# The loop over the experts of a mixture layer, with its backward branch announced at its head

## The reference

```python
N_EXPERTS = 8
TOP_K = 2
D_FF_EXPERT = 7 * D_MODEL // 2

def moe_swiglu(h, router_w, router_b, w_gate, w_up, w_down):
    logits = jnp.einsum('bsd,de->bse', h, router_w) + router_b
    top_vals, top_idx = lax.top_k(logits, TOP_K)
    top_w = jax.nn.softmax(top_vals, axis=-1)
    combine = jnp.sum(jax.nn.one_hot(top_idx, N_EXPERTS) * top_w[..., None], axis=-2)
    y = jnp.zeros_like(h)
    for e in range(N_EXPERTS):
        y = y + combine[..., e:e + 1] * swiglu(h, w_gate[e], w_up[e], w_down[e])
    return y
```

## Time and profile before

| what | us |
|---|---|
| median of 3 timed runs | 2754.07 (2751.21 to 2754.27) |
| the profiled execution | 2757.03 |
| its span, first to last instruction | 2755.2 |
| PE busy | 2518.5 (91%) |
| DVE, ACT, POOL busy | 669.3, 339.0, 58.5 |
| mixture of experts, first to last matmul | 1628 to 2744 |

### The profile page before, as it was taken

One profiled execution on the slowest core, in us unless ns is written; L12 is line 12 of the kernel. 1 busy time (PEld: TensorE's weight loads), 2 busy tenths in 40 slices (PEclk: granted clock), 3 DMA queues, 4 the chain that ended last, 5 costly groups with the idle time before them and its releaser, 6 DMA issues.

```text
span 2755.2 us, 27500 instructions
## 1 busy us (share of the span) xinstructions
PE 2518.5 (91%) x11186; PEld 1582.3 (57%) x11187; DVE 669.3 (24%) x1491; ACT 339.0 (12%) x905; POOL 58.5 (2%) x95
## 2 busy tenths in 40 slices
PE   8999899999999999999998988759998687979797
PEld 5565466656664666657776654339974343434343
DVE  0353200013532343453334621111010101010101
ACT  1242000001420000110001011001000000000001
POOL 0000000000000000000000000000000000000000
PEclk9999999999999999999999989989989898999899
DMA  5323334333234867336664279893657896759771
GB/s 209 124 96 130 141 123 153 137 128 127 92 115 168 336 244 258 116 130 260 254 269 160 81 321 431 362 407 150 262 230 317 364 429 281 304 230 403 295 309 62
DMA packets 71346, 620.35 MB, mean 225 GB/s; under 512 B 4096, under 2 KB 4096, under 8 KB 48816
## 3 DMA queue, kind: packets, MB, share of 16 engines
q1 hardware_dynamic: 57344, 557.33, 51.0%
q0 software_dynamic: 13728, 60.14, 5.7%
q10 hardware_dynamic: 144, 0.90, 0.1%
HBM read 617.31 MB, written 1.05 MB: 224 GB/s over the span
## 4 chain that ended last, share of the span: by engine, by line
PE 81%; DMA 8%; issue 5%; DVE 4%; ACT 2%; POOL 1%; ACTq 0%; DVEq 0%; POOLq 0%; SPq 0%
PE G L1907 8%; DMA big<-in_moe_pack 7%; PE S L2105 7%; PE G L1680 6%; PE S L2103 6%; PE G L1696 5%; PE S L1900 4%; PE T L1900 4%; PE G L2118 4%; PE G L1877 3%; PE S L2040 3%; PE T L2040 3%; PE G L2116 3%; PE G L2046 2%; PE G L1887 2%
## 5 line engine op out<-in xcount | busy, mean ns | idle before, releaser
L2103 PE MATMUL S<-big,hT 128*64 128x256 f32 x2240 | 280.0, 393 | 89.7 <-issue 49.7
L2103 PEld LDWEIGHTS S<-big,hT 128*64 128x64 f32 x2240 | 160.6, 140 | 206.4 <-issue 103.6
L2105 PE MATMUL S<-big,hT 128*128 128x512 f32 x448 | 206.3, 605 | 28.3 <-issue 28.3
L1555 DVE TENSOR_TENSOR probs<-S,probs 128x128 f32<-128x128 f32 (+2 forms) x105 | 35.5, 338 | 782.9 <-ACT probs L948 782.9
L1907 PE MATMUL G<-big 128*128 128x512 f32 x512 | 222.3, 592 | 0.0
L1696 PE MATMUL G<-big,hT 128*128 128x384 f32 x512 | 171.0, 488 | 0.0
L1680 PE MATMUL G<-big,hT 128*128 128x372 f32 x512 | 165.9, 488 | 2.5 <-DVE hT L1029 2.5
L1907 PEld LDWEIGHTS G<-big 128*128 128x128 f32 x512 | 97.3, 190 | 115.6 <-issue 114.8
L2105 PEld LDWEIGHTS S<-big,hT 128*128 128x128 f32 x448 | 84.6, 194 | 125.9 <-issue 125.9
L1074 DVE SCALAR_TENSOR_TENSOR big<-big,small 128x512 f32<-128x512 f32 x192 | 144.2, 751 | 6.5
L2116 PE MATMUL G<-big,pT 128*64 128x512 f32 x560 | 132.3, 593 | 8.3 <-ACT pT L953 8.3
(11 more groups left out here) (345 smaller groups left out, 2678.7 us busy)
## 6 DMA issues: line engine op xcount, KB each, us to landing
big<-in_moe_pack SPq DMA_DIRECT2D x112, 3072.0 KB, 15.9
big<-in_w_ff SPq DMA_DIRECT2D x32, 2048.0 KB, 7.8
big<-in_ada_w POOLq DMA_DIRECT2D x24, 2048.0 KB, 15.0
big<-in_ffn_pack SPq DMA_DIRECT2D x11, 3072.0 KB, 10.8
big<-in_gate_pack SPq DMA_DIRECT2D x16, 1536.0 KB, 6.4
big<-in_proj_pack SPq DMA_DIRECT2D x16, 1488.0 KB, 6.3
big<-in_branch_heads SPq DMA_DIRECT2D x6, 2048.0 KB, 7.8
big<-in_w_pack SPq DMA_DIRECT2D x8, 1536.0 KB, 6.1
```

The costliest lines, as they stand in the source:

```text
L2103: ins = mm(S[s % 2][f * FEW:(f + 1) * FEW, 0:SEQ], hTe[:, k, 0:FEW], wt[:, k, f * SEQ:(f + 1) * SEQ], start=(k == 0), stop=(k == KD - 1))
L2105: ins = mm(S[s % 2][:, :], hTe[:, k, 0:P], wt[:, k, :], start=(k == 0), stop=(k == KD - 1))
```

## The change

```diff
         def each_expert(eng, body):
 
-            with eng.Fori(0, EXPERTS) as e:
+            with nc.Fori(0, EXPERTS, engines=[eng.engine], hint_back_edge=True) as e:
                 n = eng.value_load(counts[0:1, bass.ds(e, 1)], min_val=0, max_val=SEQ)
                 widest(eng, body, e, n, 0)
```

## The result

| | before | after |
|---|---|---|
| median, us (4 runs each, same chip) | 2752.64 (2750.12 to 2754.27) | 2684.43 (2681.29 to 2686.78) |
| ratio, with its 95% interval | | 0.9752 (0.9735 to 0.9769) |
| span of the profiled execution | 2755.2 | 2684.9 |

The change makes the kernel 68.2 us faster. The forecast of 2753 missed, and so did the range (2706 to 2759). Half a sentence of its rival B ("or the head stays resident") touches what happened; it was priced at 50.5 us, and its reason "for" was another.

The account below looks back on a forecast made before the run. PE, busy 91% of the span, with 96.9 us of gaps from instruction fetches at seven passages; 1.4 us of lead less 0.6 us for the announcement gave -0.8 us from the median 2754.07: 2753 us, range 2706 to 2759.

Parts of the forecast that it names:

- rival B: Head fetched together with the foot, or still resident, so the backward branch hits: 50.5 us saved, 2712 us; chance 0.22.
- The reading of the gaps: PE's gaps at the seven passages between experts, 96.9 us, are instruction fetches at two long branches, not waits for data.
- The price of the announcement: Added instruction at the loop's head on PE: 0.08 us each, 8 times, 0.6 us; on ACT and DVE covered by idling.
- What the announcement saves depends on when the fetcher acts: At the backward branch, head and next block requested on entering the foot: lead 0.2 us, seven times, 1.4 us; chance 0.30.
- The upper bound of 50.5 us: Most the announcement could save: the backward branches' 51.1 us, less seven at the untaken branch's 0.074 us.
- Rival A: On entering the foot, the fetcher asks for the head instead of the sequential block: -9.1 us, 2745 us; chance 0.26.
- Rival C: Announcement dropped at another branch or while the body runs, so nothing happens: +0.6 us, 2754.7 us; chance 0.07.
- D: Head's block requested again at the loop's head, delaying the next block: 4 us each, 16 us slower, 2770 us; chance 0.15.
- Every microsecond off a backward branch comes off the time: PE's gaps are paid in full: one up to 7.6 us shorter moves the train of weight loads forward as much.
- a gap shortens and the expert doesn't end sooner: Sign at the passages that the forecast is wrong: it would break the reading of the idle DMA engines; no size given.

Follow-up runs that it names:

- the two padded kernels: 64 increments of an unused semaphore behind each narrow body, added to the changed kernel and to the kernel before: 2779.61 and 2783.08 us.
- the last two kernels: Kernel before, but each body on PE ends with its own backward branch, without and with announcing it at the body's head: 2670.54 and 2667.2 us.
- the kernel with slot 0 and 32 increments: Kernel before, PE's loop head on a block's first slot, plus 32 unused semaphore increments in the 64-wide body, no announcement: 2753.98 us.
- slot 48: Changed kernel with the head of PE's loop put on slot 48 of a block: 2683.12 us, ratio 0.9747.
- 84 increments: Changed kernel, PE's loop head on slot 216 of a block, plus 84 unused semaphore increments behind the 64-wide body's steps: 2785.14 us, ratio 1.012.

## Why the prediction was wrong, and where it was right

**The reading of the gaps: right.** They were fetches, not data: 65.6 of 70.3 us went with them.

**The price of the announcement: right in size.** 0.08 us was taken from the nearest branch; PE's row shows 31 to 55 ns, DVE's 47 in the median and ACT's 31. Nothing on ACT and DVE: right, shown by the kernel with the announcement on these two alone.

**"What the announcement saves depends on when the fetcher acts": the step that failed.** It priced the saving as a lead of 0.2 us at each passage (1.4 us in all, less 0.6). It counted requests at one passage and took it for granted that foot and head have to be fetched. What the runs showed in its place is a round of 9 blocks, with 8 kept, that becomes a round of 8: the fetches of foot and head go altogether at four of the seven passages, and 68.2 us with them. I had the fact that would have led on: expert 5 jumps over 1,200 instructions in 243 ns, so blocks stay, and the prediction wrote "PE keeps more than two". It didn't ask how many. The count was there to be made: 9 packets in the round of expert 4 before, shown above, for a body of 1,273 instructions that spans 6 blocks at most. A loop in which all blocks are fetched anew in each round although several are kept is a loop that is just too long, and then one block less is worth everything. The forecast's lead of 0.2 us for each passage is too small to matter beside that.

**The upper bound of 50.5 us: wrong.** It took the jump to the foot as untouched, because nothing announces it. But that jump misses for the same reason as the head, and it lost 25.8 us of its 42.7 (42.74 less 16.96). With the 41.0 us of the backward branches (51.07 less 10.07) that is 66.8 us, the gaps' 65.6 to within what else lies in them.

**Rival A** is a true mechanism where the head misses anyway. The pair alone, single for paired, was priced at 8.3 us; in the two padded kernels it took 10.9 us off the backward branches, of which 3.5 us reached the time. In this kernel it doesn't decide. **Rival B** had "the head stays resident" as half a sentence; its other half, the shared packets, was wrong, since none is sent. Its argument against, one block at a miss, holds and says nothing against residency. **Rival C** is refuted by the result and **D** too: no packet is added behind the head, and the stall after 15 matmuls is gone at the short passages.

**"Every microsecond off a backward branch comes off the time": right on the whole, and used up for the narrow experts.** The eight bodies sum to 1,013.3 us against 1,018.9. Two effects hide in that. Where a gap went, the start of the next body is quicker, because PE had not idled and the stall of 0.66 us is gone too. The first step of expert 4 before (it follows 14.35 us of idling) and after; the columns are the window, its length, busy time of PE, PEld, DVE, ACT and POOL, then the granted clock, the DMA share and GB/s:

```profile
2183.49:2190.40 6.91, 6.25 (x33) 3.63 (x33) 0.00 (x0) 0.00 (x0) 0.00 (x0) 0.61 0.60 254
```

```profile
2143.06:2146.70 3.64, 3.64 (x33) 2.31 (x33) 3.27 (x11) 0.00 (x0) 0.00 (x0) 1.00 1.01 432
```

6.91 us at a mean clock of 0.61 (most of it at the lower level, 1.2 GHz) against 3.64 us at 1.00 (2.4 GHz). The other effect goes the other way: from its first matmul to its last, expert 4 became longer, 101.9 us against 98.9, although its first step is quicker. In its window after, gap included, the DMA share is 1.00:

```profile
2143.06:2245.59 102.53, 86.61 (x617) 45.98 (x617) 14.98 (x47) 10.85 (x34) 0.00 (x0) 1.00 1.00 430
```

14 loads in 102.5 us are 7.3 us each. The 7.6 us in which the DMA engines idled are used up: the gap ahead of expert 4 shrank by 14.0 us, and the time from its first matmul to that of expert 5 by 10.5. So the prediction's sign of being wrong, "a gap shortens and the expert doesn't end sooner", didn't come, but a still shorter gap between two narrow experts would bring next to nothing: in the last two kernels the body of expert 4 takes 102.3 and 102.4 us behind no gap at all.

**The range** was too narrow on the side where the mechanism had a threshold. Both ends came from prices of one passage's packets, and none from a count of what stays.

**How many blocks stay.** The prediction wrote "more than two". The rows above show PE running rounds of 8 blocks without one fetch, and 9 fetches in a round of 9. The Trainium skill, page "Runtime: NRT & Kernel Launch", section "Instruction fetch mechanics", speaks of a window of two pages; on PE the runs don't agree with it. The same section of the Trainium skill gives PE an instruction memory of 128 KiB, refilled in blocks of 16 KiB as a FIFO; that makes 8 blocks, and with 8 the runs agree, though not with a strict order of loading, as told above. The prediction used the first of these two statements and not the second. That a taken branch to code outside what is kept forces a fetch of its target does agree, with 5.1 to 8.0 us for it beside the loads of weights.

**What stays open.** The ring is a fit to finished runs. No run was made to tell it from other rules, nor to say from which place in a block the next one is asked for, and the kernel with slot 0 and 32 increments has passages that went either way. The step from 8 blocks to 9 doesn't hang on this: it stands in the packets.

## What to carry to other kernels

When a loop's jumps miss in every round, count the blocks of a round (packets of the engine's instruction queue per round) and compare with what the engine keeps, before pricing a single fetch: near the border, one block less removes all fetches between rounds of one kind, those of other jumps too, and one more costs some 44 us here (the 62 us of the step less 18 for the increments). The block can be saved by an announcement ahead of the foot, by where the loop starts in a block, or by ending each body with its own backward branch, and the last was the best here, by 14 to 17 us between medians (of different chips). An upper bound must take in everything that shares the kept blocks, not only the branch that the change names.

## What the runs showed of the hardware

- PE kept 8 blocks of 256 instructions: a round of 8 sends no packet, one of 9 sends 9. The block used longest ago isn't the one that goes (slot 48: three loads, and the foot used just before them was gone). Nor is it strictly the one loaded first (84 increments: the foot was gone with only 5 loads behind its own). A ring written behind the running block fits all 225 branches that were replayed.
- A taken branch whose target is kept took 0.17 to 0.26 us on PE in most passages and 0.34 to 0.49 us in a few. A missed one took 2.9 to 5.0 us behind expert 2 (DMA share 0.05 there in the kernel before) and 5.1 to 8.0 us at the other passages between experts (share 0.85 to 1.04); two jumps into the wide body took 3.5 and 3.7.
- The announcement takes 31 to 68 ns on an engine. Known before the branch's block is entered, it takes the place of the request for the sequential block; two instructions ahead of the branch it does nothing.
- Increments of a semaphore that nobody waits for start 151 ns apart on PE, though the row of one shows 51 ns. 64 of them in each of five bodies cost 5.9 us a body, 92 ns each, because a part runs beside matmuls.
